# Dealing the value projection out among the indexer's score pieces, with 28 selection rounds moved later

## The reference, cut to what matters

```python
cb, cc, ch, q, k, v, qi, ki, iw = jnp.split(xn @ w_in, cuts, axis=-1)
# conv group: B * causal_dwconv3(C * h);  q, k: RMSNorm + rotary;  v: as it is
dots = jnp.einsum('bthd,bsd->bths', qi, ki)                       # indexer, 8 heads
sc   = jnp.einsum('bths,bth->bts', jax.nn.relu(dots), iw) * IDX_SCALE
_, sel = lax.top_k(where(causal, sc, -inf), 256)                  # per query row
# softmax attention over the selected keys, then one output projection
```

## Time and profile before

| what | value |
|---|---|
| median of 3 runs | 2190.65 us |
| the profiled execution, its span | 2189.5 us |
| PE busy | 2037.6 us (93%) |
| DVE busy | 973.1 us (44%) |
| ACT busy | 640.0 us (29%) |
| POOL busy | 519.4 us (24%) |

### The profile page before, as it was taken

One profiled execution on the slowest core, in us unless ns is written; L12 is line 12 of the kernel. 1 busy time (PEld: TensorE's weight loads), 2 busy tenths in 40 slices (PEclk: granted clock), 3 DMA queues, 4 the chain that ended last, 5 costly groups with the idle time before them and its releaser, 6 DMA issues.

```text
span 2189.5 us, 30040 instructions
## 1 busy us (share of the span) xinstructions
PE 2037.6 (93%) x12571; PEld 1198.0 (55%) x12571; DVE 973.1 (44%) x1633; ACT 640.0 (29%) x1315; POOL 519.4 (24%) x416
## 2 busy tenths in 40 slices
PE   6899999796977999999998999999999999999999
PEld 3523444343653556544456884444444444489998
DVE  5855999999759445615542221422222222210000
ACT  5442233443212534514223331422222222211000
POOL 1101366674103110010100012023333324142200
PEclk9856999997568557999998989999999999999999
DMA  6100113002322210020003341222121212122211
GB/s 184 38 20 14 45 39 116 22 25 89 116 97 72 82 39 1 8 92 32 29 10 101 111 133 31 82 58 59 40 58 39 58 39 61 51 91 86 90 33 31
DMA packets 132305, 132.71 MB, mean 61 GB/s; under 512 B 15294, under 2 KB 105150, under 8 KB 132132
## 3 DMA queue, kind: packets, MB, share of 16 engines
q1 hardware_dynamic: 130506, 126.33, 18.2%
q0 software_dynamic: 1664, 4.46, 0.7%
HBM read 114.78 MB, written 15.98 MB: 60 GB/s over the span
## 4 chain that ended last, share of the span: by engine, by line
PE 87%; DVE 5%; ACT 2%; POOL 2%; issue 2%; DMA 1%; SPq 0%; POOLq 0%; DVEq 0%; ACTq 0%
PE PS L1203 7%; PE PS L1205 7%; PE PS L1204 7%; PE PS L755 7%; PE PS L757 7%; PE PS L756 7%; PE PS L983 5%; PE PS L1223 4%; PE PS L1224 4%; PE PS L1225 4%; PE PS L995 2%; PE PS L872 2%; PE PS L873 2%; PE PS L874 2%; PE PS L825 2%; PE PS L826 2%
## 5 line engine op out<-in xcount | busy, mean ns | idle before, releaser
L755 PE MATMUL PS<-arena 128*128 128x512 f16 (+3 forms) x856 | 312.2, 372 | 21.4 <-POOL arena L320 14.0
L1239 ACT ACTIVATE arena<-PS 128x512 f32<-128x512 f32 (+13 forms) x365 | 176.8, 510 | 477.2 <-PE PS L757 124.6
L756 PE MATMUL PS<-arena 128*128 128x512 f16 (+3 forms) x856 | 311.1, 370 | 0.0
L757 PE MATMUL PS<-arena 128*128 128x512 bf16 (+3 forms) x856 | 310.8, 370 | 0.0
L1204 PE MATMUL PS<-arena 128*128 128x512 bf16 (+1 forms) x1056 | 303.3, 318 | 0.0
L1203 PE MATMUL PS<-arena 128*128 128x512 f16 (+1 forms) x1056 | 298.7, 318 | 0.0
L1205 PE MATMUL PS<-arena 128*128 128x512 f16 (+1 forms) x1056 | 298.5, 318 | 0.0
L320 POOL TENSOR_TENSOR arena<-arena 128x2048 bf16<-128x2048 f32 (+2 forms) x38 | 140.6, 3720 | 508.2 <-ACT arena L313 508.0
L1223 PE MATMUL PS<-arena 128*128 128x256 f16 (+1 forms) x792 | 217.2, 274 | 5.8 <-DVE arena L741 5.8
L1224 PE MATMUL PS<-arena 128*128 128x256 f16 (+1 forms) x792 | 217.0, 274 | 0.0
L1225 PE MATMUL PS<-arena 128*128 128x256 bf16 (+1 forms) x792 | 216.9, 274 | 0.0
(11 more groups left out here) (220 smaller groups left out, 3284.9 us busy)
## 6 DMA issues: line engine op xcount, KB each, us to landing
arena<-w_gu SPq DMA_DIRECT2D x44, 512.0 KB, 4.3
arena<-w_down SPq DMA_DIRECT2D x8, 1408.0 KB
arena<-w_in SPq DMA_DIRECT2D x8, 1024.0 KB, 5.2
arena<-x_prompt SPq DMA_DIRECT2D x16, 512.0 KB, 7.3
arena<-w_kv_mem SPq DMA_DIRECT2D x8, 1024.0 KB, 6.7
arena<-cache_mem_k SPq DMA_DIRECT2D x32, 256.0 KB, 2.7
arena<-cache_mem_v SPq DMA_DIRECT2D x32, 256.0 KB, 4.3
arena<-w_in SPq DMA_DIRECT2D x24, 256.0 KB, 3.8
```

Of the source, the lines that this page charges most:

```text
L755: e.matmul(out, x_hi(k)[:, cols], wh[:, q, :], start=(q == 0), stop=False)
L756: e.matmul(out, x_lo(k)[:, cols], wh[:, q, :], start=False, stop=False)
L757: mm = e.matmul(out, x_hi(k)[:, cols], wl[:, q, :], start=False, stop=(q == n - 1))
L1239: e.activation(out, in_, ACT.Copy, **kw).then_inc(sem(name), 1)
```

## The change

The value projection leaves `L4` and is cut into 72 steps (nine tiles times eight parts of the contraction, three matmuls each), dealt out behind the 48 score pieces, one and two steps in turn. It writes PSUM banks 4 to 7. ACT copies a finished tile out between two relus, POOL makes its low half. The value weights become chunk 2 and the conv chunks 3 to 6; SP stores the values before it loads chunks 4 to 8. Small indexer buffers move from the region `H` to `QK`, since the values now lie in `H` that early.

```diff
-    116, (1, 2), 7, 3, 1, 3, 1, 13, 1
+    88, (1, 2), 7, 5, 1, 3, 1, 13, 1
...
-        A_QI, A_KI, A_CONV, A_V, A_Q, A_K = 0, 1, 2, 6, 7, 8
+        A_QI, A_KI, A_V, A_CONV, A_Q, A_K = 0, 1, 2, 3, 7, 8
...
-        L4 = [("c", f, t, g) for f in range(NC_T) for t in range(3) for g in range(3)] + [("v", j) for j in range(NT)]
+        L4 = [(f, t, g) for f in range(NC_T) for t in range(3) for g in range(3)]
+        VSTEPS = NT * KT
+        def values_upto(m):
+            return VSTEPS * max(0, m + 1) // ND
+        def value_done(m):
+            return values_upto(m) // KT
...
+            def value_step(j, k):
+                if k == 0 and j == 0:
+                    A.ready(e, A_V)
+                if k == 0 and j == 2:
+                    e.wait_ge(sem("st_ev"), 2)
+                if k == 0 and j >= 4:
+                    e.wait_ge(sem("v_ev"), j - 3)
+                out = PS[0:rows(j), 4 + j % 4, :]
+                wh, wl = w_hi[A_V % 2][:, k, :], w_lo[A_V % 2][:, k, :]
+                e.matmul(out, xa_hi[:, k, tcols(j)], wh, start=(k == 0), stop=False)
+                e.matmul(out, xa_lo[:, k, tcols(j)], wh, start=False, stop=False)
+                mm = e.matmul(out, xa_hi[:, k, tcols(j)], wl, start=False, stop=(k == KT - 1))
...
                 mm.then_inc(sem("s3_mm"), 1)
+                for step in range(values_upto(m - 1), values_upto(m)):
+                    value_step(step // KT, step % KT)
             e.wait_ge(sem("idx_ld"), 16 * 2 * DEC_B * NPG)
-            e.wait_ge(sem("st_ev"), 2)
+            e.wait_ge(sem("v_ev"), NT)
...
+            def value_out(j):
+                n = rows(j)
+                e.wait_ge(sem("v_mm"), j + 1)
+                if j >= 2:
+                    e.wait_ge(sem(f"v_st{j % 2}"), 16 * (j // 2))
+                    e.wait_ge(sem("v_lo"), j - 1)
+                copy(v_f32[0:n, j % 2, :], PS[0:n, 4 + j % 4, :], "v_f32")
+                copy(v_hi[0:n, j, :], PS[0:n, 4 + j % 4, :], "v_ev")
             for m in range(ND):
+                for j in range(value_done(m - 2), value_done(m - 1)):
+                    value_out(j)
+                if m == 8:
+                    A.split_hi(e, A_CONV)
```

More of the change, by code:

```diff
@@ L562, in _ @@
                 e.dma_start(dram_rows(new_v, j), v_f32[0:rows(j), j % 2, :]).then_inc(sem(f"v_st{j % 2}"), 16)
+            for n in range(4, 9):
+                A.load(e, n)
             def key_page(n):
@@ L855, in _ @@
                     e.wait_ge(sem("s4_ev"), x - 7)
[L856 to L874, removed]
+                f, t, g = item
+                c = A_CONV + f
+                if t == 0 and g == 0:
+                    A.ready(e, c)
+                t0, tn = token_chunks()[t]
+                for k in range(KT):
+                    wh, wl = (w[c % 2][:, k, g * P:(g + 1) * P] for w in (w_hi, w_lo))
+                    xh, xl = xa_hi[:, k, t0:t0 + tn], xa_lo[:, k, t0:t0 + tn]
+                    out = PS[:, x % 8, 0:tn]
+                    e.matmul(out, wh, xh, start=(k == 0), stop=False)
+                    e.matmul(out, wh, xl, start=False, stop=False)
+                    mm = e.matmul(out, wl, xh, start=False, stop=(k == KT - 1))
                 mm.then_inc(sem("s4_mm"), 1)
@@ L1305, in _ @@
                              .rearrange("p a b -> p (a b)")[:, 0:n], ACT.Relu).then_inc(sem("s3_relu"), 1)
+            for j in range(value_done(ND - 2), NT):
+                value_out(j)
             e.wait_ge(sem("ik_tp"), 1)
@@ L1952, in sample @@
                 return v[:, SEQ:T].rearrange("p (b c) -> p b c", c=DEC_T)
-            last_of = {f: max(x for x, it in enumerate(L4) if it[0] == "c" and it[1] == f) for f in range(NC_T)}
+            A.split_lo(e, A_CONV)
+            for j in range(NT):
+                n = rows(j)
+                e.wait_ge(sem("v_ev"), j + 1)
+                e.tensor_tensor(v_lo[0:n, j, :], v_f32[0:n, j % 2, :], v_hi[0:n, j, :], ALU.subtract
+                                ).then_inc(sem("v_lo"), 1)
+            last_of = {f: max(x for x, it in enumerate(L4) if it[0] == f) for f in range(NC_T)}
             for f in range(NC_T):
@@ L1971, in _ @@
                 e.tensor_tensor(ct_lo[:, f, :], ch_s[:, 0:T], ct_hi[:, f, :], ALU.subtract).then_inc(sem("conv_lo"), 1)
-            A.split_lo(e, A_Q)
-            for j in range(NT):
-                n = rows(j)
-                e.wait_ge(sem("s4_ev"), N4C + j + 1)
-                e.tensor_tensor(v_lo[0:n, j, :], v_f32[0:n, j % 2, :], v_hi[0:n, j, :], ALU.subtract
-                                ).then_inc(sem("v_lo"), 1)
             for L in range(NI1, NI):
```

43 lines of the change are left out of this document (15 added, 28 removed).

## The result

The changed kernel takes 2204.74 us (median of 20 runs, 2190.8 to 2211.73), the kernel before beside it 2191.84: a ratio of 1.0047 (1.0031 to 1.0064), slower by 12.9 us. The forecast was 2185, faster by 6; the measured time lies inside its range (2166 to 2208), on the other side of no change. The profiled execution of the change has a span of 2207.3 us, 17.8 more than before.

What follows compares the result with a forecast made beforehand. The prediction took PE, at either clock, as the bound, and DVE's selection rounds where one stands before PE's next work. Its terms, +16.7 -7 -48 +5 +5.5 +3 +19, gave -5.8 us: 2185 us median, range 2166 to 2208.

Steps and rivals of the forecast that it cites:

- Part 1: Score pieces with value steps dealt in: clock rises after about 6 us, stage takes 91.2 us against 74.5, +16.7 us.
- Part 2: Tail between score pieces and conv: high clock lasts over ACT's copy, sample scores run faster, conv starts warm, -7 us.
- rival B: Clock rises in the dealt stage but falls before the sample group's scores: +2.4 us, 2193 us; 20%.
- Part 3: Between conv and queries: the value items leave, so the queries start right behind conv, -48.0 us.
- Parts 4 to 6: Query start behind conv +5 us; five rounds per sample pass +5.5; rounds before attention +3, behind its steps 0 to 8 +19.
- Rival A: Clock stays at 0.50 in the dealt stage: +78 us, 2269 us; 10%.
- Rival C: PE, ACT and DVE go in lockstep in the dealt stage, PE idles 15 us more: +17 us, 2208 us; 12%.
- Rival D: Late rounds are cheaper, attention's first steps would have waited anyway: -27 us, 2163 us; 13%.

Runs made afterwards that it cites:

- experiment 1: The changed kernel with 97 instead of 88 rounds ahead of the queries, so none stands behind attention's steps; 2194.59 us.
- experiment 3: The changed kernel with the old table of rounds: 116 ahead of the queries, three per sample pass; 2215.08 us.
- experiment 13: The changed kernel with 95 instead of 88 rounds ahead of the queries, three behind the last sample pass, none behind attention's steps; 2189.36 us.
- experiment 14: The changed kernel with 128 rows in the second score matmul, 95 rounds ahead of the queries, three behind the last sample pass; 2176.38 us.
- experiment 2: The kernel before with only the new table of rounds: 88 ahead of the queries, five per sample pass; 2219.03 us.
- experiment 12: The kernel before with 111 instead of 116 rounds ahead of the queries and five behind the last sample pass; 2187.11 us.
- experiment 4: The kernel before with the second score matmul of each pair over 128 rows instead of 64; 2162.23 us.
- experiment 8: The kernel before with 128 rows in the second score matmul and the first four conv items dealt into the tail; 2177.2 us.
- experiment 9: The kernel before with the first score matmul of each pair over 64 rows like the second; 2173.9 us.
- experiment 11: The kernel before with 128-row score matmuls, 111 rounds ahead of the queries, six behind the sample group, one conv item in the tail; 2164.24 us.
- experiment 7: The changed kernel with 128-row score matmuls, 95 rounds ahead of the queries, four behind the sample group, four conv items in the tail; 2194.0 us.
- experiment 15: The kernel before with 128-row score matmuls, one conv item in the tail, 111 rounds ahead of the queries, five behind the last sample pass; 2153.08 us.

## Why the prediction was wrong, step by step

The sum was -5.8 and the profiled execution shows +17.8, a miss of 23.6 us. The steps that failed are Part 1, where the fixed part of a score matmul at the high clock was taken as 0.066 us and is 0.10, and Part 2, where the clock was to last over ACT's copy and fell. Two more terms were put at nothing without a reason: the start of the score pieces, and the clock in attention. The numbers below compare one execution of each kernel.

- **Part 1, the dealt stage (+16.7).** The rise of the clock came as forecast, 6.8 us into the stage, where the forecast had about 6. The stage took 97.6 us, not 91.2. The fixed part of a score matmul was taken as 0.066 us at the high clock; over the stage a 512-column one starts 0.31 or 0.32 us ahead of the next, 0.10 more than its columns' 0.213, nearly the 0.113 of the low clock. 160 times the difference is 5.4 us, the larger part of the 6.4. I had argued that a weight load halves with the clock. The weight loads of the kernel before, in the first conv item where the clock rises, and one score load of the change at 1.00 say otherwise:

```profile
207.27 0.15 PEld L874 LDWEIGHTS PS<-arena 128*128 128x128 bf16 x1 [0.28 <-issue]
207.57 0.10 PEld L872 LDWEIGHTS PS<-arena 128*128 128x128 f16 x1
...
203.22 0.09 PEld L854 LDWEIGHTS PS<-arena 64*128 64x128 f16 x1 [0.23 <-issue]
```

Conv's covered loads go from 0.15 to 0.10 us, and the uncovered score loads only from 0.10 (121.15 in the kernel before) to 0.09.
- **Part 1, the start.** The first score matmul came 4.3 us later, which the sum does not have. In the nine profiles without dealing it came at 104.0 to 107.1, in the eight with it at 106.9 to 109.6; what delays it was not tested.
- **Part 2, the tail (-7).** It was -1.4. The clock fell, which is rival B: it is 1.00 until 211 us, through PE's two waits on ACT, and 0.52 from there to 227, over the sixteen matmuls, 1.07 us apart as before. But it is neither always so nor never: of the seven profiles with dealing and no filler the clock stayed at 1.00 in four (experiments 1, 3, 13, 14), where the tail takes 14.4 us (-7.9; the forecast had -6.6 for it and -2.8 for a warm conv start, which experiments 1, 3 and 13 have too: 132.7 us from the first conv matmul to the last instead of 135.5), and fell in three. The change and experiments 1, 3 and 13 have the same instructions up to the end of the tail, so the difference lies in the execution; why it falls in some is open. In the six without dealing or filler it was low each time. The two lengths differ by 6.5 us, a part of the 21 us over which the change's times spread. A miss of 5.6 here.
- **Part 3, the value items (-48), with Parts 4 to 6 (+32.5).** As a sum they were right: from the first conv matmul to step 9 the change saves 13.0 us, the forecast said 15.5. Single terms: conv to queries +5 as said, with a wait of 9.8 us; sample passes +5.3 for 5.5; step 0 +2.9 for 3; steps 0 to 8 +21.8 for 19. The first eight steps were cheaper than forecast, 2.98 to 3.18 us where 3.4 was said; the excess is the mark, 3.94 us for 0.69. A miss of 2.5.
- **Attention's clock (not in the sum).** It rose at about 870 us instead of 845, which costs 5. It rises early (step 9 to the end in 1465 us) in six of the 17 profiles and late (1470 to 1474) in eleven; the kernel before with other tables (experiments 2 and 12) is among the late ones. It is late in seven of the eight with dealing and in four of the nine without. No kernel was profiled twice, so it stays open whether it belongs to the execution alone or the change has a part in it; the one of the kernel before that I worked from was an early one. That accounts for 4.8 of the 23.6. The profiled run of the change was also 4.3 us above the median of its runs, which is most of the distance between +17.8 in the profile and +12.9 in the medians.

4.3 + 6.4 + 5.6 + 2.5 + 4.8 = 23.6.

What the steps hid is the frame. I named the rounds as a second bound, but booked -48 as a gain of PE's that was then taxed. With the table of the kernel before, DVE's list sets how long it is from the first round to step 9: the five kernels that have it (before, 3, 4, 8, 9) have lists of 510.7 to 513.2 us, with PE's work between them different by up to 47 us. That does not mean that DVE never rests there: it is busy for 438.5 of the 513.2 us before, 182.6 of the 190.6 up to the first query item, and waits for PE and ACT in the sample group. Read in this way the sum is two terms, first round +26 and list -13, where the forecast comes to +9.7 and -15.5, and the first question is what stands ahead of the first round. Before, said the same: DVE is busy 45.27 of the 46.90 us of the value items, so they covered rounds and not the reverse.

Rival A is dead (the clock rose). Rival C named the right sign and a near time, 2208, by the wrong way: there is no lockstep in the dealt stage, where PE is busy for 95.3 of 97.6 us. Rival D is dead: the late rounds and the mark cost 21.8 us, and without them steps 0 to 8 of experiment 1 take 20.7 less.

The Trainium skill's page "TensorE: Matmul & The Clock Gate" was weighed in the prediction. Its Part 2 says that weight loads are pulled ahead of running matmuls. Experiment 4 agrees where both matmuls have 128 rows (121.54 for a matmul at 121.75); the kernel before disagrees where 128 and 64 rows follow each other (121.15 for one at 121.16). Its Part 1 says that a busy PE gets the high clock. Experiment 9 disagrees: its score pieces are all over 64 rows, and PE was busy for 47.5 of 52 us at 0.50.

## What to carry to other kernels

Before moving work between two stages, mark for each engine the point from which it hardly rests, and read the change as two numbers: how much later that point comes, and how much shorter the engine's own list becomes. Work that is dealt into another engine's gaps ahead of that point can cost the bound engine nearly its full length: in experiment 8, 20.7 us of conv made the first round 18.5 us later. One item instead of four (experiment 11) did not make it later. When an engine is at 0.50 and wholly busy, look at the shapes in its rows before adding work to it: here one operand slice, 64 rows made 128, was worth 29 us, and dealing nothing. An idle stretch in which rounds are to be put has a wait at its end; see in the timeline on which side of it the new work would stand.

## What the runs showed of the hardware

- A matmul whose number of rows differs from the one before it costs 0.113 us more at the low clock and 0.10 at the high one, at any width seen (128 to 512 columns); its weight load starts with it instead of one matmul ahead (121.15 for 121.16). In pairs of equal rows, 128 (experiment 4) or 64 (experiment 9), there is no such part. In one place of the change it stands between equal rows: in the last value tile the weights have 64 columns, and the score matmul behind it, whose weights have 128, comes 0.31 us later (202.59, 202.90), four times over.
- In the score pieces PE stays at 0.50 for 74.5 us of uninterrupted matmuls of 128 and 64 rows in turn, and for 52 us of matmuls of 64 rows. With 128 rows throughout, the same stage is at 0.96 with PE busy for 37.63 of 45.40 us, and with value matmuls among the mixed pairs at 0.97.
- A DVE tensor_scalar over 128x1024 f32 took 0.69 us in fourteen profiles and 3.93 or 3.94 us in the three where a POOL tensor_tensor ran beside it. What they share was not tested.
- The same instructions can get either clock: the tail behind the dealt stage took 20.9 us or 14.4, and the attention stretch from step 40 to 48 took 29.8 to 29.9 us in six profiles and 34.5 to 37.6 in eleven. Kernels whose tail held 128-row matmuls of the conv list had the high clock there in every profile (experiments 7, 8, 11, 15), in experiment 8 after 3 us at the low one, and the runs of each lie within 6 us.
